# Gate and up products of the experts 2 to 15 in halves, as seven products each

## What is computed

```python
def expert_choice_ffn(h, w_router, w_gate, w_up, w_down):
    t = h.reshape(N, D)
    cap = CAPACITY_FACTOR * N // N_EXPERTS
    aff = jax.nn.softmax(jnp.matmul(t, w_router).astype(jnp.float32), axis=-1)
    gate, idx = lax.top_k(aff.T, cap)
    xe = t[idx]
    hid = jax.nn.silu(jnp.einsum('ecd,edf->ecf', xe, w_gate)) * jnp.einsum('ecd,edf->ecf', xe, w_up)
    ye = jnp.einsum('ecf,efd->ecd', hid, w_down) * gate[..., None].astype(hid.dtype)
    out = jnp.zeros((N, D), ye.dtype).at[idx.reshape(-1)].add(ye.reshape(-1, D))
```

## Time and profile before

| | |
|---|---|
| median of 3 runs | 1682.34 us |
| the 3 runs | 1682.12 to 1683.62 us |
| the profiled execution | 1680.82 us |
| its span in the trace | 1679.0 us |
| granted clock of TensorE over the span, mean | 0.997 |
| TensorE busy, matmuls | 1650.2 us (98%) |
| weight loads busy | 1421.4 us (85%) |

### The profile page before, as it was taken

One profiled execution on the slowest core, in us unless ns is written; L12 is line 12 of the kernel. 1 busy time (PEld: TensorE's weight loads), 2 busy tenths in 40 slices (PEclk: granted clock), 3 DMA queues, 4 the chain that ended last, 5 costly groups with the idle time before them and its releaser, 6 DMA issues.

```text
span 1679.0 us, 25780 instructions
## 1 busy us (share of the span) xinstructions
PE 1650.2 (98%) x10397; PEld 1421.4 (85%) x10397; DVE 505.8 (30%) x1111; ACT 404.4 (24%) x926; POOL 506.8 (30%) x465
## 2 busy tenths in 40 slices
PE   9999999999999999999999999999999999999996
PEld 6556698866898864456999999999999999999996
DVE  5575344673313640089111110111011110111105
ACT  3335134323312434454011011110111011110115
POOL 0073132532231444442132223323233122322220
PEclk9999999999999999999999999999999999999998
DMA  9311113321111627433678779887788778787794
GB/s 303 92 54 39 38 39 84 90 78 55 38 32 51 189 73 270 126 109 132 235 246 316 238 233 296 259 295 234 246 281 291 261 235 282 243 317 237 232 322 191
DMA packets 189812, 309.83 MB, mean 185 GB/s; under 512 B 12644, under 2 KB 77972, under 8 KB 189616
## 3 DMA queue, kind: packets, MB, share of 16 engines
q1 hardware_dynamic: 171840, 283.30, 49.0%
q0 software_dynamic: 17904, 25.62, 7.6%
HBM read 275.82 MB, written 33.07 MB: 184 GB/s over the span
## 4 chain that ended last, share of the span: by engine, by line
PE 91%; DVE 5%; ACT 1%; issue 1%; DMA 1%; POOL 0%; SPq 0%; DVEq 0%; ACTq 0%; POOLq 0%
PE bank L2473 33%; PE bank L2490 16%; PE bank L2186 9%; PE bank L2213 8%; PE bank L2377 5%; PE bank L2106 3%; PE bank L2142 2%; PE bank L2234 2%; PE bank L2307 2%; PE bank L2288 2%; DVE arena L1875 1%; DVE arena L1873 1%; DVE arena L1877 1%; PE bank L2152 1%; PE bank L2150 1%; PE bank L2510 1%
## 5 line engine op out<-in xcount | busy, mean ns | idle before, releaser
L2473 PE MATMUL bank<-arena 128*128 128x164 f32 x4096 | 573.0, 303 | 0.2 <-DVE arena L1982 0.2
L2473 PEld LDWEIGHTS bank<-arena 128*128 128x128 f32 x4096 | 570.8, 190 | 0.3 <-DVE arena L1982 0.3
L2490 PE MATMUL bank<-arena 128*128 128x164 f32 x1920 | 269.6, 303 | 0.0
L2490 PEld LDWEIGHTS bank<-arena 128*128 128x128 f32 x1920 | 268.0, 190 | 0.0
L973 POOL DMA_INDIRECT residual<-arena,cur_scatter x90 | 140.7, 1564 | 180.0 <-ACT arena L1455 157.2
L1992 DVE TENSOR_TENSOR arena<-bank,arena 128x328 f32<-128x328 f32 x64 | 32.0, 500 | 527.5 <-ACT arena L1444 509.9
L2186 PE MATMUL bank<-arena 128*128 128x400 f32 (+1 forms) x560 | 158.5, 445 | 0.0
L2186 PEld LDWEIGHTS bank<-arena 128*128 128x128 f32 x560 | 106.2, 190 | 51.7
L2377 PE MATMUL bank<-arena 128*128 128x512 f32 x320 | 146.0, 599 | 0.8 <-issue 0.7
L1444 ACT ACTIVATE arena<-bank 128x328 f32<-128x328 f32 x64 | 28.4, 444 | 479.3 <-PE bank L2473 457.4
L2213 PE MATMUL bank<-arena 128*128 128x192 f32 x840 | 137.7, 325 | 0.2 <-ACT arena L1014 0.2
(11 more groups left out here) (277 smaller groups left out, 1597.6 us busy)
## 6 DMA issues: line engine op xcount, KB each, us to landing
arena<-in_w_up SPq DMA_DIRECT2D x32, 2048.0 KB, 14.0
arena<-in_w_down SPq DMA_DIRECT2D x32, 2048.0 KB
arena<-in_w_gate SPq DMA_DIRECT2D x32, 2048.0 KB, 7.9
arena<-in_w_in SPq DMA_DIRECT2D x7, 1536.0 KB, 7.4
arena<-in_x_sample SPq DMA_DIRECT2D x14, 512.0 KB, 6.3
arena<-x_features_first SPq DMA_DIRECT2D x11, 512.0 KB, 8.3
arena<-decay_rows SPq DMA_DIRECT2D x22, 256.0 KB, 4.7
arena<-state_rows SPq DMA_DIRECT2D x44, 128.0 KB, 4.3
```

The source lines that it names most:

```text
L2473: last = pe.matmul(ps[2 * w + fp % 2][:, a * SLOTS:(a + 1) * SLOTS], ring[2 * (fp // 2) + w][:, k, f * P:(f + 1) * P], xeT[:, k, 0:SLOTS], ...
L2490: last = pe.matmul(result_tiles(4 + dp % 2)[:, a, 0:SLOTS], ring[4 + dp // 2][:, k, dt * P:(dt + 1) * P], hidT[:, k, :], start=k == 0, sto ...
```

## The change

With D the features and F the outputs, both weight matrices of an expert are cut into four quarters (A11, A21 the upper and lower features of the first output half, A12, A22 of the second), and the 164 tokens into two halves of 82 slots (B11, B12 the upper features, B21, B22 the lower). Seven products of quarters take the place of eight, in the form of Strassen and Winograd. Each product is 4 x 4 blocks with 82 columns (`halved_product`): 16 matmuls of the program. They are called A1, B, E1, F1, E2, F2, A2, where the same letter is the same bank of accumulators.

- TensorE: 7 x 16 = 112 matmuls for gate and 112 for up, of 82 columns, where there were 64 and 64 of 164. `down` keeps its 64, with the order of the blocks turned (lower half first).
- DVE: four sums of token halves (T1 to T4), four sums of quarters of the gate weights (S1 to S4, 128 x 2048 each; S3 in place), ten sums that join the products, four multiplications of gate and up, where there were four multiplications of 128 x 328. Three of the weight sums of the next expert stand between the `turn_results` of this one.
- POOL: the four sums of the up weights (`up_sums`), between `gather` and `scatter`, after a wait for the slots 3 and 1 and for the first product of this expert.
- ACT: copies A1 out, Silu in four quarters.
- SP: the slots are loaded in the order 2, 0, 3, 1, 4, 5, each after the last product that reads it; for expert 2 in the order 0, 2, 1, 3.
- Ahead of the experts only names of semaphores change: the loads of the gate biases and of the convolution's weights share one (`vectors_in`, DVE waits for all six at L1583, PE too), the three loads of the router share one, and the carries.

Expert 1 and expert 16 are computed as before.

```diff
+        HALVED = range(1, NE - 1)
+        def halved(at):
+            return arena[:, at:at + 4 * HS].rearrange("p (f s) -> p f s", f=4)
+        def expert_sum(n):
+            return arena[:, 11 * D + n * 2048:11 * D + (n + 1) * 2048].rearrange("p (k n) -> p k n", k=4)
+        token_sums = [halved(n * 4 * HS) for n in range(4)]
+        shared_part = [halved((4 + w) * 4 * HS) for w in range(2)]
+        gates = arena[:, 9136:9136 + KT * SLOTS].rearrange("p (k s) -> p k s", k=KT)
+        EXPERT_BANKS = ({"A": 0, "B": 1, "F": 2, "E": 3}, {"A": 5, "B": 4, "F": 6, "E": 7})
+        EXPERT_PHASES = ("A1", "B", "E1", "F1", "E2", "F2", "A2")
...
+        def expert_weights(w):
+            return ring[w][:, 0:4, :], ring[w][:, 4:8, :], ring[2 + w][:, 0:4, :], ring[2 + w][:, 4:8, :]
...
-                with sp.Fori(0, NE - 1) as i:
-                    for s in range(6):
-                        done = (gu_full, 2) if s < 2 else (gu_full, 4) if s < 4 else (dn_full, 2 * (s - 3))
-                        sp.wait_ge(done[0], i * 4 + done[1])
-                        sp.dma_start(ring[s], expert_source(s, bass.ds(i + 1, 1))).then_inc(slot_in[s], 16)
+                def reload(s, e):
+                    sp.sem_inc(passed, 1)
+                    sp.dma_start(ring[s], expert_source(s, bass.ds(e, 1))).then_inc(slot_in[s], 16)
+                for s in (0, 2, 1, 3, 4, 5):
+                    if s < 4:
+                        sp.wait_ge(gu_full, 4 if s > 1 else 2)
+                    else:
+                        sp.wait_ge(dn_full, 2 * (s - 3))
+                    sp.dma_start(ring[s], expert_source(s, slice(1, 2))).then_inc(slot_in[s], 16)
+                with sp.Fori(0, NE - 2) as i:
+                    for w in range(2):
+                        sp.wait_ge(products, product_count(i + 1, w, "E2"))
+                        reload(2 + w, i + 2)
+                        sp.wait_ge(products, product_count(i + 1, w, "A2"))
+                        reload(w, i + 2)
+                    for s in (4, 5):
+                        sp.wait_ge(dn_full, i * 4 + 4 + 2 * (s - 3))
+                        reload(s, i + 2)
...
+                def up_sums(e):
+                    a11, a12, a21, a22 = expert_weights(1)
+                    s1, s2, s4 = (expert_sum(3 + n) for n in range(3))
+                    for s in (3, 1):
+                        pool.wait_ge(slot_in[s], e * 16 + 16)
+                        pool.sem_inc(passed, 1)
+                    pool.wait_ge(products, (e - 1) * 14 + 1)
+                    pool.tensor_tensor(s1, a21, a22, ALU.add).then_inc(sums_ready, 1)
+                    pool.wait_ge(sums_ready, up_sum_count(e, 1))
+                    pool.tensor_tensor(s2, s1, a11, ALU.subtract).then_inc(sums_ready, 1)
+                    pool.tensor_tensor(a21, a11, a21, ALU.subtract).then_inc(sums_ready, 1)
+                    pool.wait_ge(sums_ready, up_sum_count(e, 2))
+                    pool.tensor_tensor(s4, a12, s2, ALU.subtract).then_inc(sums_ready, 1)
...
                     gather(i + 2, i * 2 + 1)
+                    up_sums(i + 1)
                     scatter(i, i * 2 + 2)
...
+                def halved_gates(e):
+                    act.wait_ge(products, product_count(e, 0, "A1"))
+                    act.activation(shared_part[0], expert_part(0, "A"), ACT.Copy).then_inc(activated, 1)
+                    for x, rows, cols_ in (("C22", LOWER, TWO_), ("C21", LOWER, ONE), ("C12", UPPER, TWO_)):
+                        act.wait_ge(combined, combo_count(e, x + "_0"))
+                        act.activation(gates[:, rows, cols_], gates[:, rows, cols_], ACT.Silu).then_inc(activated, 1)
+                    act.wait_ge(products, product_count(e, 0, "A2"))
+                    act.activation(gates[:, UPPER, ONE], expert_part(0, "A"), ACT.Silu).then_inc(activated, 1)
+                    act.wait_ge(products, product_count(e, 1, "A1"))
+                    act.activation(shared_part[1], expert_part(1, "A"), ACT.Copy).then_inc(activated, 1)
...
+                def halved_expert(e):
+                    weight_sum_four(e, 0)
+                    shared(e, 0)
+                    with_e(e, 0, gates)
+                    lower_two(e, 0, gates)
+                    lower_one(e, 0, gates)
+                    upper_two(e, 0, gates)
+                    shared(e, 1)
+                    with_e(e, 1, hidT)
+                    lower_two(e, 1, hidT)
+                    gated_half(e, "C22", LOWER, TWO_, "C22_1")
+                    lower_one(e, 1, hidT)
+                    gated_half(e, "C21", LOWER, ONE, "C21_1")
+                    upper_two(e, 1, hidT)
+                    gated_half(e, "C12", UPPER, TWO_, "C12_1")
+                    dve.wait_ge(activated, activated_count(e, "C11"))
+                    dve.wait_ge(products, product_count(e, 1, "A2"))
+                    dve.tensor_tensor(hidT[:, UPPER, ONE], expert_part(1, "A"), gates[:, UPPER, ONE], ALU.mult).then_inc(combined, 1)
+                def results_and_next(e, more=True):
+                    turn_rows(e + 1)
+                    if more:
+                        token_halves(e + 1)
+                    turn_results(e, 0)
+                    if more:
+                        weight_sum_one(e + 1, 0)
+                        weight_sum_two(e + 1, 0)
+                    turn_results(e, 1)
+                    if more:
+                        weight_sum_three(e + 1, 0)
+                    turn_results(e, 2)
+                    turn_results(e, 3)
...
+                def halved_product(e, w, x, weights, tokens):
+                    to = expert_part(w, x[0])
+                    for f in range(4):
+                        for k in range(4):
+                            last = pe.matmul(to[:, f, :], weights[:, k, f * P:(f + 1) * P], tokens[:, k, :], start=f + k == 0 and x[1:] != "2",
+                                             stop=k == 3, skip_group_check=True)
+                    last.then_inc(products, 1)
...
+                def halved_products(e, w):
+                    a11, a12, a21, a22 = expert_weights(w)
+                    s1, s2, s4 = (expert_sum(3 * w + n) for n in range(3))
+                    t1, t2, t3, t4 = token_sums
+                    if w == 0:
+                        pe.wait_ge(rows_turned, e)
+                    pe.wait_ge(slot_in[w], e * 16 + 16)
+                    halved_product(e, w, "A1", a11, xeT[:, UPPER, ONE])
+                    wait_sum(e, w, 2)
+                    halved_product(e, w, "B", s2, t2)
+                    wait_sum(e, w, 3)
+                    halved_product(e, w, "E1", a21, t3)
+                    halved_product(e, w, "F1", s1, t1)
+                    pe.wait_ge(combined, combo_count(e, f"E{w}"))
+                    halved_product(e, w, "E2", a22, t4)
+                    pe.wait_ge(combined, combo_count(e, f"C22_{w}"))
+                    wait_sum(e, w, 4)
+                    halved_product(e, w, "F2", s4, xeT[:, LOWER, TWO_])
+                    pe.wait_ge(activated, activated_count(e, f"A{w}"))
+                    halved_product(e, w, "A2", a12, xeT[:, LOWER, ONE])
...
                 with pe.Fori(0, NE - 2) as i:
+                    for w in range(2):
+                        halved_products(i + 1, w)
                     for m in range(4):
-                        down(i, m)
-                    for m in range(4):
-                        gate_up(i + 1, m)
+                        down(i + 1, m)
                 for m in range(4):
-                    down(NE - 2, m)
-                for m in range(4):
-                    gate_up(NE - 1, m)
+                    gate_up(NE - 1, m, 1)
```

182 lines of the change are left out of this document (132 added, 50 removed).

## The result

The changed kernel took 1885.2 us (median of four runs, 1883.73 to 1887.01), beside 1682.98 us for the kernel before on the same chip: a ratio of 1.1202, 95% interval 1.1183 to 1.1222. In another session it was 1884.57 us (five runs), ratio 1.1193 (1.1178 to 1.1207). It is slower by 202 us; the forecast of 1878 us lay 7 us low. The profiled execution took 1885.95 us, its span is 1884.2 us; before, the span was 1679.0 us. The difference to explain is thus 205.2 us.

What follows compares the result with a forecast made beforehand. TensorE alone was taken to bound the experts' stage, with block loads setting the pace of short matmuls. 1680.8 + 193 for gate and up + 3 for waits = 1877, plus 1.5 to the median: 1878 us, range 1857 to 1910.

Steps and rivals of the forecast that it cites:

- What bounds the stage: Experts' stage, 820 to 1621 us: PE busy for all 801 us, so TensorE alone sets the stage's end.
- What a short matmul costs: Gate and up: each 128-column load holds the stream about 110 ns; at 110.3 ns, 13.8 us more an expert, 193 in all.
- Down and the first and last expert: TensorE's down, and experts 1 and 16: unchanged, down staying at 17.81 us.
- Waits inside the products: Semaphores at 14 new product boundaries: no wait found, 0.2 us an expert allowed, 3 us in all, bounds 0 and 14.
- DVE: Weight sums 2.4 us each, 23 us of 67 an expert in all; hidden with at least 2.5 us to spare.
- POOL: Four up-weight sums of 4.9 us each, ending at 23.4 us after gate's start, scatter by 37; hidden behind TensorE.
- the rival of late sums: POOL's sums take 10.2 us each, so up's E1 waits 2.3 us in 14 experts: 32 us, 1910 us in all; 6%.
- The DMAs: Weight loads in the experts: same traffic over 67 us, share from 0.80 to about 0.64; slots land in time.
- Merged semaphores: Loads ahead of the experts that are now waited for together: no cost.
- Hidden loads: Gate and up: next block loads while the current matmul streams, distance 70 ns, saving 54 to 62 us: 1625 us; 3%.
- partly hidden ones: Gate and up: every other load hidden, say, distance 90 ns, +66 us: 1750 us; 3%.
- The clock: Products of gate and up: TensorE falls to 1.2 GHz, each distance doubles, 692 us more: 2570 us; 2%.

Runs made afterwards that it cites:

- x1_block64: Changed kernel with each half product loading only 64 of a block's 128 output columns, 82 still streamed: 1642.6 us, ratio 0.9757.
- x2_stream128: Changed kernel with 128 token columns streamed in each half product instead of 82, loaded block still 128 columns: 1885.86 us.
- x4_semaphores: Kernel before with only the change's merged semaphores: 1682.57 us against 1682.69, ratio 1.0001.
- x5_no_weight_sums: Changed kernel with DVE's and POOL's eight weight sums of an expert narrowed to 8 columns instead of 512 of each block: 1883.99 us, ratio 1.1197.
- x6_two_halves: Kernel before with every 164-column matmul of gate and up split into two of 82: 2026.24 us profiled, 2083.0 us in the other execution.
- x10_two_halves_again: Kernel before with gate and up matmuls as two of 82 columns, six more executions: four at 2025.96 to 2026.18 us, two at 2080.8 and 2079.7.

## Why the prediction was right, by its own steps

- **What bounds the stage.** Right. PE is busy throughout the stage, and all that the stage adds is TensorE's. After the first matmul of the experts, up to the end of expert 15, no releaser has any time on PE, and one has 0.2 us on its loads (DVE's L2104).
- **What a short matmul costs.** The mechanism was right and is now shown by taking the block in half (x1_block64) and by varying what is streamed (64, 82 and 128 columns, the same 111.6 to 111.7 ns). The size was a little off: I took 110.3 ns, nearer to the two loads beside 16-column matmuls than to the long stream of loads in the earlier trace rows, since there the loaded block was the identity. The stream's 111.6 ns was the right one; 75 distances are a better measure than two, and what the block holds changed nothing. That term gave 193 us and measured 14 x 14.36 = 201.0 us, inside its bounds of 182 to 204. One reading on the way was inexact: at 635 us the load that starts at 635.44 did not wait for the 512-column matmul to get under way. That matmul is the second of this row, and the first of 16 columns already follows it at 635.44:

```profile
634.58 1.02 PE L2377 MATMUL bank<-arena 128*128 128x512 f32 x2
```

  The load started together with the 16-column matmul. That TensorE is one load ahead there follows all the same.
- **The Trainium skill's page "TensorE: Matmul & The Clock Gate".** Its section "LDWEIGHTS (loading the stationary operand)" gives 107 ns for 128 columns and agrees to 5 ns. Its "Back-to-back issue gap" of some 81 ns for a pair at 128 columns does not hold here: x2_stream128 is such a stream of pairs, in fp32, at 111.7 ns.
- **Down and the first and last expert.** Predicted unchanged at 17.81 us; 17.85 us, 0.6 us over 14 experts.
- **Waits inside the products.** I allowed 3 us for 14 new boundaries an expert and bounded it by 0 and 14; it was 0. The 448 matmuls of an expert have no idle time at any boundary, and their distance is that of the stream in the earlier trace rows, which has no boundaries in it.
- **DVE.** A weight sum took 2.25 to 2.30 us (predicted 2.4), and the sums between the results of down cost TensorE 0.2 us in all, in expert 1's down; at most 1 us was predicted for it.
- **POOL.** The price was taken from the 1040-column row (4.9 us for 2048 columns) against the 512-column one (10.2 us):

```profile
1139.36 4.51 POOL L1052 TENSOR_TENSOR arena<-arena 128x2048 f32<-128x2048 f32 x1 [7.10 <-PE bank L2698]
1143.94 4.52 POOL L1054 TENSOR_TENSOR arena<-arena 128x2048 f32<-128x2048 f32 x1
1148.41 4.53 POOL L1055 TENSOR_TENSOR arena<-arena 128x2048 f32<-128x2048 f32 x1
1152.90 4.52 POOL L1057 TENSOR_TENSOR arena<-arena 128x2048 f32<-128x2048 f32 x1
```

They end 21.9 us after gate's start at 1135.57, where 23.4 was predicted. The last issue of the scatter ends at 1169.50, 33.9 us after gate's start (predicted 37), so the rival of late sums did not come. Its premise was weaker than stated. The 1040-column row is L743, an operation of the mixer on tokens and not on weight quarters. And of the weight sums ahead of the experts, which do read quarters in blocks, it took the slowest; two others of the same form lie at 2.2 to 2.5 ns a column:

```profile
L775 POOL TENSOR_TENSOR arena<-arena 128x512 f32<-128x512 f32 x4 | 5.1, 1276 | 33.0 <-PE bank L2224 16.8 <-DVEq L1680 15.8 <-POOL arena L787 0.5
L777 POOL TENSOR_TENSOR arena<-arena 128x512 f32<-128x512 f32 x4 | 4.4, 1111 | 0.3
```

  In x1_block64, where an expert has some 50 us and not 67.8, the weight sums did cost time, but in another place than the rival named: down waited, not the products of up.
- **The DMAs.** The share of 0.65 is the one predicted (0.64), and up's weights land after 7.8 us and gate's after 11.2, where the earlier trace rows has 14.0 and 7.9.
- **Merged semaphores.** Predicted nothing, measured nothing (x4_semaphores).
- **Ahead of the experts.** Nothing was predicted, and in the profiled execution they start at 809.43 us instead of 806.09, 3.3 us later. Two short stretches have a lower clock, both in front of the changed code. Here is the first of them as a window of the kernel before, of the changed kernel (with the second stretch, 802 to 806 us, under it) and of x4_semaphores:

```profile
146.00:153.50 7.50, 7.27 (x46) 4.65 (x47) 6.24 (x5) 3.99 (x13) 4.61 (x3) 1.00 0.09 7
```

```profile
146.00:153.50 7.50, 7.27 (x45) 4.51 (x44) 5.74 (x5) 3.99 (x14) 4.18 (x3) 0.78 0.09 6
802.00:806.00 4.00, 4.00 (x23) 4.00 (x23) 0.51 (x1) 1.28 (x1) 1.07 (x2) 0.57 0.57 170
```

```profile
146.00:153.50 7.50, 7.26 (x43) 4.46 (x42) 6.10 (x5) 3.99 (x13) 4.54 (x3) 0.77 0.09 7
```

x4_semaphores has the first dip too in its profiled execution and still the kernel before's median, and in x5_no_weight_sums, which has the changed kernel's order ahead of the experts, both stretches are at 1.00 and the experts start at 806.79. So the dips are not shown to come from the change. Single executions differ by such amounts (the kernel before's lie between 1681.19 and 1687.4 us within one session). The account of the profiled difference is 201.6 for the periods, 0.2 for the sums, 3.3 here, and about 0.1 for the rest: 205.2 us.

The medians differ by 202.2 us where the forecast said 193 + 3 over 1682, and 1885.2 lies in the range of 1857 to 1910. Of the 7 us missed, +8 are the distance and -3 the waits allowed and not taken, so that two errors partly cancel. Of the +2 left, 0.6 are down's, 0.2 the sums' and 1.0 is the kernel before, 1682.98 here where the forecast took 1682; the rest is not told apart from the scatter between runs.

**The rivals.** Hidden loads (1625 us) and partly hidden ones (1750 us) fall with the distance of 111.6 ns, which none of the streams of 128-column blocks read here undercuts. Late sums: not here, though sums do cost time beside shorter products. The clock: not in the changed kernel, whose mean is 0.995 or more in all nine executions, but real at 41 and 16 columns, and with a mean of 0.97 in three of eight executions of x6_two_halves and x10_two_halves_again, which stream 82. The prediction's argument against it, that the earlier trace rows stays at the fast level, could not carry that much: two of the matmuls there have 16 columns, the others 128.

No kernel here that computes the result beats the kernel before. Seven half products need 7/4 as many matmuls, each with its block load, as the whole ones; at 111.6 ns each that is 195 ns for each matmul of full width, and a full-width matmul of this kernel takes 139. By 139.2 ns for 164 columns the two are level at about 230 columns (an estimate from these two numbers, not tried). In the mixer the half products are wide enough to hide the load. Its group of 192 columns takes 164 ns for each (137.7 us over 840), well over 111.6; whether the seven products pay there was not tried either.

```profile
L2213 PE MATMUL bank<-arena 128*128 128x192 f32 x840 | 137.7, 325 | 0.2 <-ACT arena L1014 0.2
```

## What to carry to other kernels

Before cutting matmuls into smaller ones, look in the trace for the distance of the starts in a stretch where loads stand densely: that is the floor for each loaded block, and streaming saved below it gives no time back. Count the loads of the new form, not its multiplications; a form with 7/8 of the arithmetic and 7/4 of the loads can pay only where a matmul streams long enough to hide them. And take the floor from the longest run of equal distances, not from a pair that stands alone.

## What the runs showed of the hardware

- At a granted clock of 1.00 a stream of fp32 matmuls with a block of 128 columns for each runs at 111.6 to 111.7 ns for 64, 82 or 128 columns streamed, at about 112 ns for 16 (over 3.5 us), and at 139 ns for 164; with a block of 64 columns and 82 streamed, at 71 ns.
- The granted clock can fall while PE and PEld read busy for 100% of the time: 0.53 over an expert's products that stream 41 or 16 columns for each loaded block of 128, and 0.50 in their middle, against 1.00 in the traces with 64, 82 and 128. Dense loads show as busy time, and did not keep the clock at the higher level there. It cost 604 to 608 us, three times what the change itself cost.
- POOL's issues of the gather, an indirect DMA, take 0.94 to 1.03 us alone and 1.9 to 2.4 us when they start beside a large fp32 sum of DVE.
- POOL adds two fp32 tiles of 2048 columns in 4.51 us, DVE in 2.27 us. POOL's 2.2 ns a column lies near the 1040-column row (2.4) and far from its 512-column row (5.0).
